# High parts of a chunk ahead of the modulation rows, and earlier sums of weights, in the second feed-forward pass of a float32 block pair

## The reference, cut to what matters

```python
# first block, feed-forward (D_FF = 2816, 22 tiles of 128)
h = rmsnorm(x, g_ffn)
u = einsum("bsd,df->bsf", h, w_up)
f_gate = causal_dwconv(u[..., :D_FF], conv_f_w) + conv_f_b      # 3 taps
f = gelu(f_gate) * u[..., D_FF:]
x = x + einsum("bsf,fd->bsd", f, w_down)
...
# second block, made ready meanwhile
mod   = silu(c)     @ w_mod + b_mod
mod_c = silu(c_ctx) @ w_mod + b_mod
hc = rms(ctx, norm_g) * (1 + scale_c) + shift_c
```

## Time and profile before

| | |
|---|---|
| median of three runs | 2100.38 us (2100.0 to 2101.67) |
| profiled execution | 2099.9 us |
| its span, first to last instruction | 2097.4 us |
| TensorE matmul busy | 1998.9 us, 95% |
| VectorE, ScalarE, GpSimd busy | 62%, 27%, 41% |
| mean granted clock of TensorE | 0.984 |
| combined products (L826) in the span | 665.7 to 1053.1 us |
| down products in the span | 1054.6 to about 1380 us |

### The profile page before, as it was taken

One profiled execution on the slowest core, in us unless ns is written; L12 is line 12 of the kernel. 1 busy time (PEld: TensorE's weight loads), 2 busy tenths in 40 slices (PEclk: granted clock), 3 DMA queues, 4 the chain that ended last, 5 costly groups with the idle time before them and its releaser, 6 DMA issues.

```text
span 2097.4 us, 25341 instructions
## 1 busy us (share of the span) xinstructions
PE 1998.9 (95%) x9557; PEld 1659.7 (79%) x9557; DVE 1293.6 (62%) x1288; ACT 572.1 (27%) x747; POOL 854.9 (41%) x576
## 2 busy tenths in 40 slices
PE   6999999999999999999987798999999999999998
PEld 5888788888887888888866677888788878888887
DVE  4999995312549888898875655545443745556520
ACT  4000001301233333333321000243222234555411
POOL 2444355444326555555564434523122511112221
PEclk9999999999999999999999998999999999999999
DMA  4211111231111222222263323211123210000033
GB/s 135 60 40 50 40 45 46 66 112 53 41 51 60 81 90 84 66 90 90 79 241 131 120 86 106 71 31 41 31 77 94 77 39 1 11 11 1 1 131 90
DMA packets 188879, 145.29 MB, mean 69 GB/s; under 512 B 10036, under 2 KB 171777, under 8 KB 188801
## 3 DMA queue, kind: packets, MB, share of 16 engines
q1 hardware_dynamic: 180608, 129.26, 19.8%
q10 hardware_dynamic: 8192, 14.94, 2.3%
HBM read 124.25 MB, written 19.92 MB: 69 GB/s over the span
## 4 chain that ended last, share of the span: by engine, by line
PE 79%; DVE 8%; issue 4%; POOL 4%; ACT 3%; DMA 1%; ACTq 0%; SPq 0%; POOLq 0%; DVEq 0%
PE ps L607 48%; PE ps L826 18%; PE ps L1056 2%; POOL wlo L519 1%; DVE prob L2238 1%; POOL xb_lo L542 1%; PE ps L1073 1%; PE ps L1070 1%; PE ps L1067 1%; PE ps L1064 1%; PE ps L1089 1%; PE ps L1091 1%; PE ps L1090 1%; PE ps L1076 1%; PE ps L879 1%
## 5 line engine op out<-in xcount | busy, mean ns | idle before, releaser
L516 POOL TENSOR_TENSOR small<-ones 128x1 f32<-128x1 f32 x126 | 46.0, 365 | 769.1 <-PE ps L607 706.8
L519 POOL TENSOR_TENSOR wlo<-raw,whi 128x1024 fp32r<-128x1024 f32 (+1 forms) x122 | 337.1, 2763 | 10.2
L607 PE MATMUL ps<-xa_hi,whi 128*128 128x512 f32 x992 | 315.9, 397 | 22.0 <-POOL wlo L519 12.6
L607 PE MATMUL ps<-xa_lo,whi 128*128 128x512 f32 x992 | 310.5, 392 | 0.0
L607 PE MATMUL ps<-xa_hi,wlo 128*128 128x512 f32 x992 | 309.7, 391 | 0.0
L607 PE MATMUL ps<-xb_hi,whi 128*128 128x512 f32 x768 | 241.5, 396 | 27.4 <-POOL wlo L519 20.8
L607 PE MATMUL ps<-xb_lo,whi 128*128 128x512 f32 x768 | 238.2, 392 | 0.0
L607 PE MATMUL ps<-xb_hi,wlo 128*128 128x512 f32 x768 | 237.7, 391 | 0.0
L607 PEld LDWEIGHTS ps<-xa_hi,whi 128*128 128x128 f32 x992 | 184.7, 189 | 64.9 <-issue 16.5
L607 PEld LDWEIGHTS ps<-xa_lo,whi 128*128 128x128 f32 x992 | 187.6, 189 | 39.5
L607 PEld LDWEIGHTS ps<-xa_hi,wlo 128*128 128x128 f32 x992 | 187.4, 189 | 39.6
(11 more groups left out here) (373 smaller groups left out, 3508.0 us busy)
## 6 DMA issues: line engine op xcount, KB each, us to landing
raw<-in_w_in SPq DMA_DIRECT2D x52, 512.0 KB, 3.8
t<-in_w_mod ACTq DMA_DIRECT2D x48, 256.0 KB, 2.8
f_scratch<-t SPq DMA_DIRECT2D x22, 512.0 KB, 2.7
raw<-in_w_down SPq DMA_DIRECT2D x22, 512.0 KB, 3.5
raw<-in_w_up SPq DMA_DIRECT2D x40, 256.0 KB, 3.6
w_raw<-in_w_up SPq DMA_DIRECT2D x40, 256.0 KB, 3.7
f_raw_a<-f_scratch SPq DMA_DIRECT2D x5, 1024.0 KB, 5.9
x_columns<-in_x SPq DMA_DIRECT2D x8, 512.0 KB, 5.1
```

Source lines behind the costliest of these rows:

```text
L516: nc.gpsimd.tensor_tensor(small[:, 106 + slab.slot:107 + slab.slot], ones[:, 0:1], ones[:, 0:1], ALU.mult)
L519: nc.gpsimd.tensor_tensor(lo, src, f32(hi), ALU.subtract).then_inc(split_done, 1)
L607: ins = mm(dst[j], w, r[j], start=first and f, stop=last and l)
```

## The change

Three things, all of them order.

1. ScalarE: the high parts of chunk 1 are made ahead of the first modulation rows, those of chunk 2 right behind the first four rows, both ahead of the context's squares. Those of chunks 3, 4 and 5 wait for the rows up to rows_until(1, 1), (3, 0) and (4, 1). GpSimd makes the low parts of chunk 5 behind the third slab of chunk 4 instead of the second.
2. Low parts of chunk 0: GpSimd makes 0 and 3 instead of 0 and 1; VectorE makes 1 and 2, inside the last comb_pair ahead of its taps, instead of 2 and 3 behind it.
3. The last classical product signals b12_read behind its fourth k of eight. The first weight_sums on VectorE move up to that point, ahead of token_low(3), and ScalarE makes the high part of weight piece 2 then instead of at the end of the product.

```diff
         def f_low(c):
             hi, lo = f_parts(c)
-            for k in range(2 if c == 0 else f_tiles(c)):
+            for k in (0, 3) if c == 0 else range(f_tiles(c)):
...
-                        if k == 1 and c < NDC - 1:
+                        if k == (2 if c == NDC - 2 else 1) and c < NDC - 1:
                             f_low(c + 1)
...
+                if read is not None and k == read[0]:
+                    last.then_inc(read[1], 1)
...
-        for k in range(2, 4):
-            gemm(J + k, L + k, XBh, XBl, KD, w8)
+        gemm(J + 2, L + 2, XBh, XBl, KD, w8)
+        gemm(J + 3, L + 3, XBh, XBl, KD, w8, read=(3, sem("b12_read")))
...
-            if k < 2:
-                pe.wait_ge(sem("f_lo"), k + 1)
+            if k in (0, 3):
+                pe.wait_ge(sem("f_lo"), k // 3 + 1)
             else:
-                pe.wait_ge(sem("tc_dve"), k + 5)
+                pe.wait_ge(sem("tc_dve"), k + 6)
...
         weight_hi(0, 1)
+        act.wait_ge(sem("b12_read"), 1)
+        weight_hi(0, 2)
         act.wait_ge(job_done, JOBS["ffn"] + 4)
-        weight_hi(0, 2)
         weight_hi(0, 3)
...
+        f_hi(1, range(4))
         mod_rows(range(0, 4))
+        f_hi(2, range(4))
...
         for c in range(NDC):
-            if 1 <= c:
-                rows_until(c - 1, 3)
+            if c >= 3:
+                rows_until(*{3: (1, 1), 4: (3, 0), 5: (4, 1)}[c])
                 f_hi(c, range(f_tiles(c)))
...
+        rows_until(4, 7)
         for m in range(KD):
...
             step(tt(T[2][:, 0:S], T[2][:, 0:S], rbc[:, :], ALU.mult))
+            if following is None:
+                for k in (1, 2):
+                    dve.wait_ge(sem("f_hi"), k + 1)
+                    tt(f_parts(0)[1][:, k, :], fraw[FSLOT[0]][:, k, :], f32(f_parts(0)[0][:, k, :]), ALU.subtract).then_inc(sem("tc_dve"), 1)
             taps(t)
...
         first_gate(1)
+        dve.wait_ge(sem("b12_read"), 1)
+        weight_sums(0, 0)
         token_low(3)
         first_tap(1)
         taps(1)
         first_up(1)
-        dve.wait_ge(job_done, JOBS["ffn"] + 4)
-        weight_sums(0, 0)
         first_product(1)
...
-        for k in (2, 3):
-            dve.wait_ge(sem("f_hi"), k + 1)
-            tt(f_parts(0)[1][:, k, :], fraw[FSLOT[0]][:, k, :], f32(f_parts(0)[0][:, k, :]), ALU.subtract).then_inc(sem("tc_dve"), 1)
         dve.wait_ge(sem("c_sq"), 2)
```

More of the change, by code:

```diff
@@ L614, in gemm @@
         def gemm(job, slab, rh, rl, kts, wcol, new_slab=True, n=1024, each_k=None, waited=KD, order=None,
-                 col0=0, p=P, begins=1, weights=None, between=None):
+                 col0=0, p=P, begins=1, weights=None, between=None, read=None):
             if job.n or job.c >= 2:
```

## The result

The changed kernel takes 2083.01 us (median of four, 2080.3 to 2084.31), the kernel before in the same rounds 2101.03. The ratio is 0.9913, interval 0.9896 to 0.993. The forecast was 2083. The profiled execution took 2084.31 us, the slowest of the four, with a span of 2081.6; I read stretches from it and totals from the medians.

A forecast was written before the change was run, and what follows sets the result against it. TensorE, busy 95% of the span, was taken as the bound, so its idle time could be won. -38.9 + 1.0 + 14.7 + 2.3 + 3.6 = -17.3 us from the 2100.4 median gave 2083, own range 2077 to 2089.

The forecast's parts named there:

- Part 1: ScalarE's high parts ahead of the modulation rows in the second feed-forward pass: -38.9 us, with +1 us charged for late VectorE.
- The three waits: TensorE idle of 7.75, 13.02 and 11.80 us at the fifth tile of chunks 1, 2 and 3, all expected to go.
- The crowding: Chunks 1 to 3: VectorE late, accumulating while GpSimd makes low parts; charged +1 us for the three together.
- Part 2: Chunk 0: context squares wait behind chunk 2's high parts, so TensorE starts m = 2 at 1088.4, not 1073.65: +14.7 us.
- forecast landing of 1079.6: Time the load f_raw_c, needed by chunk 2's high parts, was taken to land, as of old; bounds 1077 and 1082.6.
- the removed wait of 4.61 us: TensorE's wait at the third k of chunk 0: goes, but no gain, TensorE only comes sooner to the longer wait.
- The slow stretch: Matmuls at the lower clock behind the new wait at m = 2 of chunk 0: +2.3 us.
- Part 3: Weight sums at half of the last classical product: first_up(1) comes later, n = 2 starts at 678.4, +3.6 us.
- the context chain hidden: Rival: no new wait at m = 2 of chunk 0 and its old wait gained, 2059 us in all; chance 0.07.
- crowding: Rival: accumulations, low parts and splits cost TensorE 4 us in each of three chunks, 2094 us; chance 0.14.
- the waits staying: Rival: chunks 2 and 3 keep their waits at the fifth tile, 29.5 us come back, 2112 us, slower; chance 0.07.
- the start gaining: Rival: GpSimd's turns don't hold up first_up(1) ahead of n = 2, -3.3 instead of +3.6, 2076 us; chance 0.10.

The follow-up runs named there:

- e3: Changed kernel with the high parts of chunks 3 to 5 waiting for the old rows again and f_low(5) behind the second slab: 2109.49 us, ratio 1.0038.
- e5: Changed kernel with first_up(1) directly behind the early weight sums, ahead of token_low(3), first_tap(1) and taps(1): 2075.49 us, ratio 0.9873.
- e2: Changed kernel with the context's two squares and their root on ScalarE ahead of f_hi(1), the four rows and f_hi(2): 2065.85 us, ratio 0.983.
- e4: Changed kernel with chunk 0's low parts as of old, GpSimd 0 and 1, VectorE 2 and 3 behind the last pair: 2081.11 us, ratio 0.9909.
- e1: Changed kernel with the first weight sums and the high part of weight piece 2 back behind the last classical product: 2083.18 us, ratio 0.9908.
- e6: Changed kernel with GpSimd's split of weight piece 3, and all behind it, held back until first_up(1) has run: 2081.84 us, ratio 0.9901.
- e9: Changed kernel with VectorE's part of the context behind down(0, 3) instead of ahead of down(0, 0): 2066.71 us, ratio 0.9837.
- e7: Changed kernel with first_up(1) directly behind the sums, and the context's squares ahead of the last gelu, root right behind it: 2055.83 us, ratio 0.9788.
- e8: Changed kernel with 25 matmuls of constants on TensorE between tiles 1 and 2 of chunk 0: 2079.94 us, ratio 0.9905.

## Why the prediction was right

**Part 1** held. The three waits went (-36.8 between the marks against -38.9 + 1). e3 shows the cause for two of them: put the rows back and they return at the same length. The crowding that I charged at 1 us is the 0.48 at 1244.46 and, in this execution, 1.6 us of lower clock behind it; where the clock stayed up (e5 and four others) the same stretch would give -38.4. f_hi(4), the tightest, was in time by less than a microsecond.

**Part 2** held in mechanism and size: +15.7 against +14.7, and +14.3 to +14.6 by the five other profiles with this code. The forecast landing of 1079.6 did not yet hold the late start of the stage; with the 2.4 us that chunk 0 started later it is 1082.0, and the load landed at 1083.2. From there the steps were as in the sum: two high parts, 1.9 us, and 6.72 from the first square to m = 2 against 6.75. I had the load landing where it landed of old, although it was asked for later, and the profiles bear that out; that older transfers had drained is my reason and is not shown. e2 takes the chain away and gets 17.2 us back. That the removed wait of 4.61 us is no gain, e4 shows: it returns, and m = 2 comes no later. The slow stretch, forecast at 2.3 us, was 1.3 in this execution and 2.0 to 2.6 in e1, e3, e5 and e6. Both terms together were +17.1 against +17.0; that their errors of +1.0 and -0.9 cancel is luck of this one profile.

**Part 3** held in mechanism and at the mark: +3.7 against +3.6, with GpSimd's turns measured by e6 and first_up(1) as the condition by e5. I took five turns of 1.28 us, 6.4, and there were six that cost 6.1 together: the count and the price of one were off, and the two errors cancel. What I didn't foresee is that 1.3 us came back at once, since the clock rose at about 681.6 where it had risen at 680.5 of old, though n = 2 began 3.7 later; so the start of chunk 0 lost only 2.4, and the total of e1 doesn't resolve even that.

The rivals: the context chain hidden is excluded by the 23.64 us, crowding and the waits staying by the marks of chunks 1 to 3, the start gaining by 678.46. The total agrees better than its parts. The errors of the marks, +0.1, -1.3, +1.0, -0.9, +1.1 and +1.7 us, sum to +1.7, and the profiled execution lay 1.3 above the median. The interval of the ratio is some 3.6 us either way, so that 2083 was met to the microsecond is luck; that it was met within a few is not.

## What to carry to other kernels

When work is put ahead on an engine that runs in order, list what it is put ahead of and follow each item to the engine that waits for it: here four high parts that nobody needed for 50 us stood ahead of two small squares that held TensorE. A removed wait is worth nothing if the next one ends at the same time, so find the next condition of the same instruction first (first_up(1) for n = 2, down(0, 0) for m = 2). A piece of work moved on VectorE must be priced with GpSimd's turns at its new place. And before a microsecond is explained, look at the same stage in other profiles with the same code: here that took the explanation away from two differences of 1 us.

## What the runs showed of the hardware

VectorE and GpSimd shut each other out for whole instructions when both work from SBUF, and the loss is the sum of the other's turns: a sum of 0.69 us took 3.30 behind a long low part, four instructions took 8.6 us with GpSimd at work and 5.7 without (e6), and two of 1.42 us together took 4.71 (e9). VectorE's first_up(1), which reads one of its operands from PSUM, took 1.21 us in e5 with GpSimd's splits under way and 1.22 in the changed kernel without them.

TensorE's lower clock behind a short wait is not fixed. Behind 3.3 us of idle the granted clock was 0.50 in the kernel before and 1.00 throughout 640 to 700 us in e1. Behind the wait of 0.48 us in chunk 3 it fell to 0.50 in the changed kernel and four other profiles and stayed at 1.00 in five, which is 1.6 us. Behind waits of 4.60 us and more, the one with fillers apart, it was 0.50 every time here. At m = 2 of chunk 0 it then cost from 1.3 us (behind 23.64) to 2.8 (behind 4.88, e7).

The load f_raw_c did not land sooner for being asked for sooner, while the DMA engines were busy (share 1.03 and 409 GB/s over 1074 to 1077 us in the kernel before). Its last part was asked for 11.5 us behind the start of chunk 0 in the kernel before, 11.6 in e4 and 13.7 to 13.8 in e1, e3, e5, e6 and e8, and landed 24.7 to 25.0 us behind it in all of these. In the changed kernel's profile it landed at 26.2, and why is open.
